# One block for experts and final sums, and three reorderings before it, in a streaming mixer and mixture-of-experts layer

## What is computed

```
m, s_h, s_r, buf = parallel_mixers(rmsnorm(h))     # HGRN2 scan + RWKV-7 scan, gated and added
h = h + m @ w_out
h = h + memory_cross_attention(rmsnorm(h), mem_k, mem_v)
h = h + hier_moe(rmsnorm(h))                       # best of 4 groups, then 2 of its 8 experts
y = rmsnorm(h)
```

## Time and profile before

| What | Value |
|---|---|
| median of 3 runs | 1563.61 us (1563.08 to 1565.07) |
| profiled execution: its time / its span | 1564.5 us / 1562.8 us |
| PE busy / PEld | 1418.8 us (91%) / 1183.2 us (76%) |
| DVE / ACT / POOL busy | 644.7 us (41%) / 576.9 us (37%) / 150.2 us (10%) |
| mean granted TensorE clock | 0.955 of full speed |

### The profile page before, as it was taken

The page is one execution under the profiler, slowest core; times in us unless marked ns, Lnnn a source line. Parts: engine busy times, 40 slices in busy tenths (PEclk is TensorE's granted clock), DMA queues, the critical chain, the costliest instruction groups (busy, mean ns, idle before and its releaser), DMA issues. The chain is left out here.

```text
span 1562.8 us, 35890 instructions
## 1 busy us (share of the span) xinstructions
PE 1418.8 (91%) x16169; PEld 1183.2 (76%) x16169; DVE 644.7 (41%) x955; ACT 576.9 (37%) x813; POOL 150.2 (10%) x265
## 2 busy tenths in 40 slices
PE   4899999897999999799999979999998599999980
PEld 3899999887999999699999969998887233333330
DVE  4333333573566566434445436532333222222224
ACT  4454554421656665324343364433325000000002
POOL 1000000100200010000000000000000133333410
PEclk8899999998999999899999989999998699999995
DMA  4233333301233232300000142562213699999834
GB/s 160 55 95 81 91 86 85 99 2 48 80 87 86 81 101 81 108 4 10 4 4 4 49 144 80 172 183 69 82 55 135 255 398 400 377 392 390 331 117 180
DMA packets 168271, 205.56 MB, mean 132 GB/s; under 512 B 24477, under 2 KB 148086, under 8 KB 155574
## 3 DMA queue, kind: packets, MB, share of 16 engines
q1 hardware_dynamic: 152722, 187.72, 35.2%
q0 software_dynamic: 15088, 15.46, 3.0%
q10 hardware_dynamic: 308, 0.09, 0.0%
HBM read 242.55 MB, written 27.23 MB: 173 GB/s over the span
## 5 line engine op out<-in xcount | busy, mean ns | idle before, releaser
L273 PE MATMUL ps<-rounded,w_hi 128*128 128x272 f32 (+1 forms) x1200 | 351.4, 293 | 23.6 <-DVE w_lo L262 16.6
L274 PE MATMUL ps<-rounded,w_hi 128*128 128x272 f32 (+1 forms) x1200 | 349.2, 291 | 0.0
L275 PE MATMUL ps<-rounded,w_lo 128*128 128x272 f32 (+1 forms) x1200 | 348.3, 290 | 0.0
L273 PEld LDWEIGHTS ps<-rounded,w_hi 128*128 128x128 f32 (+1 forms) x1200 | 227.7, 190 | 30.8 <-issue 30.3
L275 PEld LDWEIGHTS ps<-rounded,w_lo 128*128 128x128 f32 (+1 forms) x1200 | 227.3, 189 | 0.3
L274 PEld LDWEIGHTS ps<-rounded,w_hi 128*128 128x128 f32 (+1 forms) x1200 | 226.9, 189 | 0.6
L262 DVE TENSOR_TENSOR w_lo<-ring,w_hi 128x1024 fp32r<-128x1024 f32 (+1 forms) x75 | 90.7, 1214 | 181.7 <-ACT w_hi L257 181.7
L257 ACT CAST w_hi<-ring 128x1024 fp32r<-128x1024 f32 (+1 forms) x75 | 77.6, 1038 | 147.9 <-DMA ring<-in_w_in 147.8
L1497 PE MATMUL ps<-rounded,d_high 128*128 128x272 f32 x384 | 114.7, 299 | 6.7 <-DVE rounded L1417 5.8
L1498 PE MATMUL ps<-rounded,d_high 128*128 128x272 f32 x384 | 112.7, 294 | 0.0
L1499 PE MATMUL ps<-rounded,d_low 128*128 128x272 f32 x384 | 112.3, 293 | 0.0
(11 more groups left out here) (411 smaller groups left out, 2312.7 us busy)
## 6 DMA issues: line engine op xcount, KB each, us to landing
ring<-in_w_in SPq DMA_DIRECT2D x74, 512.0 KB, 3.9
arena<-in_expert_w_gate SPq DMA_DIRECT2D x32, 1024.0 KB, 8.0
arena<-in_expert_w_up SPq DMA_DIRECT2D x32, 1024.0 KB, 10.4
arena<-in_expert_w_down SPq DMA_DIRECT2D x32, 1024.0 KB, 10.4
arena<-in_w_out SPq DMA_DIRECT2D x8, 512.0 KB, 4.6
arena<-in_wk_x SPq DMA_DIRECT2D x8, 512.0 KB, 3.9
arena<-in_wv_x SPq DMA_DIRECT2D x8, 512.0 KB, 4.1
arena<-in_wq_x SPq DMA_DIRECT2D x8, 512.0 KB, 3.9
```

What stands on the lines that cost most here:

```text
L273: pe.matmul(out, w_hi[j][:, k, 0:m], xh, start=(k == 0), stop=False)
L274: pe.matmul(out, w_hi[j][:, k, 0:m], xl, start=False, stop=False)
L275: mm = pe.matmul(out, w_lo[j][:, k, 0:m], xh, start=False, stop=(k == FT - 1))
```

## The change

Five edits:
- **Scan end.** In the last scan step ScalarE copies u0 before it does `rstd` of the chunk before. After the scan, the transposed end state goes to PSUM bank 4 in place of bank 0, TensorE then does the first half of dense unit 1 before it waits for the last chunk, and ScalarE copies the end state before it splits the last chunk.
- **Norm factors.** The memory norm, "x" and "f" are now one Sqrt on ScalarE and a reciprocal on VectorE; a one-element Sqrt after attention has the table loaded there.
- **Token counting.** `count_tokens` stands after the third `turn_row` in TensorE's order, not after the fifth.
- **First gathers.** The three gathers leave the long block (with GpSimd's wait for `x_out`) and open GpSimd's part of the expert block.
- **One block.** The final block's work follows the expert work in the same block: no `end_stage` between, and SP, not GpSimd, waits for the scatters.

```diff
@@ scan_act
-            if i >= 1:
+            if i >= 1 and nxt:
                 rstd(act, i - 1)
             if cur:
                 keep_bank("r_u0_done", n, C_B, u0_s, "r_u0")
-                if not nxt:
-                    for u in range(1, HIS):
-                        d_hi(act, u)
+            if not nxt:
+                rstd(act, i - 1)
+                for u in range(1, HIS):
+                    d_hi(act, u)
@@ d_unit
             if u == 1:
                 pe.wait_ge(S["r_st0"], K)
-                pe.wait_ge(S["r_state_turned"], 2)
+                d_steps(pe, u, 1).then_inc(S["d_prod"], 1)
+                return
@@ norm factors
-        def token_rstd(act, rs, b, name):
+        def token_rms(act, rs, b, name):
...
-                act.activation(dst, src, ACT.Ln, scale=1.0 / D, bias=eps).then_inc(S[name + "_ln"], 1)
-            act.wait_ge(S[name + "_ln"], 2)
-            for dst, src, eps in parts:
-                act.activation(dst, dst, ACT.Exp, scale=-0.5).then_inc(S[name + "_rs"], 1)
+                act.activation(dst, src, ACT.Sqrt, scale=1.0 / D, bias=eps).then_inc(S[name + "_rms"], 1)
+
+        def token_inverse(dve, rs, name):
+            dve.wait_ge(S[name + "_rms"], 2)
+            for m, ts in ((P, slice(0, TT - 1)), (DEC, slice(TT - 1, TT))):
+                dve.reciprocal(rs[0:m, ts], rs[0:m, ts]).then_inc(S[name + "_rs"], 1)
@@ long block, GpSimd
-                pool.wait_ge(S["x_out"], 16 * TT)
                 pool.wait_ge(S["x_from"], 1)
-                for i in range(XR):
-                    gather_x(pool, i)
@@ long block, ScalarE
                 rstd(act, K - 1)
+                act.wait_ge(S["r_end_turned"], 2)
+                act.copy(st_vk[1], heads(4)).then_inc(S["r_state_turned"], 1)
                 split_out_act(act, K - 1)
-                act.wait_ge(S["r_end_turned"], 2)
-                act.copy(st_vk[1], heads(Z_B)).then_inc(S["r_state_turned"], 1)
...
-                act.activation(mem_rs, mem_ss, ACT.Ln, scale=1.0 / D, bias=eps_c).then_inc(S["mem_ln"], 1)
-                act.wait_ge(S["mem_ln"], 1)
-                act.activation(mem_rs, mem_rs, ACT.Exp, scale=-0.5).then_inc(S["mem_rs"], 1)
+                act.activation(mem_rs, mem_ss, ACT.Sqrt, scale=1.0 / D, bias=eps_c).then_inc(S["mem_rms"], 1)
...
                         attention_act(act)
+                        act.activation(tiny[:, 3:4], eps_c, ACT.Sqrt)
@@ long block, TensorE
                 pe.wait_ge(S["r_st"], K)
+                turn_heads(pe, 4, st_p).then_inc(S["r_end_turned"], 1)
+                pe.wait_ge(S["d_lo"], 2)
                 pe.wait_ge(S["r_z"], K)
-                turn_heads(pe, Z_B, st_p).then_inc(S["r_end_turned"], 1)
+                d_steps(pe, 1, 0)
                 pe.wait_ge(S["r_out_lo"], K)
                 d_steps(pe, 0, 1).then_inc(S["d_prod"], 1)
...
-                for t in range(TT):
+                for t in range(3):
                     turn_row(pe, t)
                 count_tokens(pe)
+                for t in range(3, TT):
+                    turn_row(pe, t)
@@ long block, VectorE
                 split_out_dve(dve, K - 1)
+                dve.wait_ge(S["mem_rms"], 1)
+                dve.reciprocal(mem_rs, mem_rs).then_inc(S["mem_rs"], 1)
...
+                        token_inverse(dve, x_rs, "x")
...
+                token_inverse(dve, f_rs, "f")
@@ expert block
             def _(sp):
...
+                for j in range(2):
+                    sp.wait_ge(S[f"m_out{j}"], 16 * (PAIRS // 2))
+                for t in range(TT):
+                    m = tokens(t)
+                    sp.dma_start(res[t][0:m], y_picks.rearrange("(k n) d -> n k d", k=TOP_K)[t * P:t * P + m]).then_inc(S[f"y_in{t}"], 16)
...
             def _(pool):
+                for i in range(XR):
+                    gather_x(pool, i)
...
                 scatter_y(pool, PAIRS - 1)
-                for j in range(2):
-                    pool.wait_ge(S[f"m_out{j}"], 16 * (PAIRS // 2))
...
-        S.end_stage()
-
-        with nc.Block() as block:
```

More of the change, by code:

```diff
@@ L1646, in att_out @@
             if t == 0:
-                pe.wait_ge(S["x_ln"], 2)
+                pe.wait_ge(S["x_rms"], 2)
             else:
@@ L1986, in _ @@
                         act.wait_ge(S["sq_summed"], 1)
-                        token_rstd(act, x_rs, 7, "x")
+                        token_rms(act, x_rs, 7, "x")
                 act.wait_ge(S["logits"], 1)
@@ L1990, in _ @@
                 act.wait_ge(S["sq_summed"], 2)
-                token_rstd(act, f_rs, 5, "f")
+                token_rms(act, f_rs, 5, "f")
                 act.wait_ge(S["f_rs"], 2)
@@ L2338, in keep_y @@
             dve.tensor_copy(y_b[i % 2].rearrange("p (c n) -> p c n", c=2), ps[:, 5:7, :]).then_inc(S["m_y"], 1)
+        froom = Room(flat[:, 0:B4 * BW], B4 * BW)
+        res = [froom.take(TOP_K, D) for _ in range(TT)]
+        y_sq, ss, rstd = froom.take(D), froom.take(TT), froom.take(TT)
         with nc.Block() as block:
@@ L2348, in _ @@
                         load_part(sp, u - 2, "d")
+                for j in range(2):
[3 more added lines that the diff above has]
+                    sp.dma_start(res[t][0:m], y_picks.rearrange("(k n) d -> n k d", k=TOP_K)[t * P:t * P + m]).then_inc(S[f"y_in{t}"], 16)
+                for t in range(TT):
+                    sp.wait_ge(S["y_done"], t + 1)
+                    dst = O["y_prompt"][0, t * P:(t + 1) * P, :] if t < TT - 1 else O["y_sample"][0]
+                    sp.dma_start(dst, h_tok[0:tokens(t), t, :]).then_inc(S["y_out"], 16)
+                sp.wait_ge(S["y_out"], 16 * TT)
             @block.gpsimd
             def _(pool):
+                for i in range(XR):
+                    gather_x(pool, i)
                 for i in range(PAIRS):
@@ L2371, in _ @@
                     keep_h(act, i)
+                for t in range(TT):
+                    m = tokens(t)
+                    act.wait_ge(S["y_sum"], 2 * t + 2)
+                    act.activation(y_sq[0:m], h_tok[0:m, t, :], ACT.Square, accum_out=ss[0:m, t:t + 1]).then_inc(S["y_ss"], 1)
+                    act.wait_ge(S["y_ss"], t + 1)
+                    act.activation(rstd[0:m, t:t + 1], ss[0:m, t:t + 1], ACT.Sqrt, bias=eps_c[0:m], scale=1.0 / D).then_inc(S["y_rms"], 1)
             @block.tensor
@@ L2396, in _ @@
                     keep_y(dve, i)
-        S.end_stage()
-        froom = Room(flat[:, 0:B4 * BW], B4 * BW)
-        res = [froom.take(TOP_K, D) for _ in range(TT)]
-        y_sq, ss, rstd = froom.take(D), froom.take(TT), froom.take(TT)
-        with nc.Block() as block:
-            @block.gpsimd
-            def _(pool):
-                pass
-            @block.vector
-            def _(dve):
                 dve.wait_ge(S["slot_gain_in"], 16)
@@ L2431, in _ @@
                                                  op0=ALU.mult, op1=ALU.mult).then_inc(S["y_done"], 1)
-            @block.scalar
-            def _(act):
-                for t in range(TT):
-                    m = tokens(t)
-                    act.wait_ge(S["y_sum"], 2 * t + 2)
-                    act.activation(y_sq[0:m], h_tok[0:m, t, :], ACT.Square, accum_out=ss[0:m, t:t + 1]).then_inc(S["y_ss"], 1)
-                    act.wait_ge(S["y_ss"], t + 1)
-                    act.activation(rstd[0:m, t:t + 1], ss[0:m, t:t + 1], ACT.Sqrt, bias=eps_c[0:m], scale=1.0 / D).then_inc(S["y_rms"], 1)
-            @block.sync
-            def _(sp):
-                for t in range(TT):
-                    m = tokens(t)
-                    sp.dma_start(res[t][0:m], y_picks.rearrange("(k n) d -> n k d", k=TOP_K)[t * P:t * P + m]).then_inc(S[f"y_in{t}"], 16)
-                for t in range(TT):
-                    sp.wait_ge(S["y_done"], t + 1)
-                    dst = O["y_prompt"][0, t * P:(t + 1) * P, :] if t < TT - 1 else O["y_sample"][0]
-                    sp.dma_start(dst, h_tok[0:tokens(t), t, :]).then_inc(S["y_out"], 16)
-                sp.wait_ge(S["y_out"], 16 * TT)
 _INS = ["x_prompt", "x_sample", "mem_prompt", "cache_mem_k", "cache_mem_v", "state_hgrn", "state_rwkv", "state_rwkv_shift",
```

## The result

The changed kernel takes 1550.98 us (median of 4 runs, 1549.71 to 1552.09), the kernel before 1563.34 us on the same chip (1562.69 to 1565.07): ratio 0.9919, 95% interval 0.9902 to 0.9936. It is faster, by 12.4 us where 15.6 were forecast (1548.0, range 1541.5 to 1554.5). The profiled execution took 1550.33 us, its span is 1548.5, 14.3 less than before.

A forecast was written before the change was run, and what follows sets the result against it. TensorE was taken to set the pace between four places of waiting; -5.75 - 3.4 + 3.0 - 9.5 = -15.65 us from the median of 1563.61 gave 1548.0 us, range 1541.5 to 1554.5.

The forecast's parts named there:

- Scan end: End of the scan: earlier second correction and unit 1 matmuls done inside TensorE's wait, together -5.75 us.
- four places: Scan end, router, border to the experts and border behind them: -5.75, -3.4, +3.0 and -9.5 us.
- Rival 1: Border to the experts: first gather lands as in a quiet stretch, -0.8 for +3.0, 1544.2 us; chance 0.17.
- rival 2: Router block's end: GpSimd's drain of 6.9 us stays though the gathers leave, 1552.6 us; chance 0.15.
- rival 3: First expert pairs: TensorE starts at half clock and stays there, slower, 1592 us with four pairs; chance 0.03.
- the order: Last scan step: u0 copied before `rstd` brings the second correction and everything to the last chunk's split 2.7 us earlier.
- unit 1's half: Scan end: 24 matmuls of dense unit 1 hidden in TensorE's wait for the last chunk's split, 3.05 us.
- Router: Router: norm factor starts VectorE's chain 1.3 us earlier, counting starts after three row tiles; together -3.4 us up to VectorE's end.
- The "bounds" of -1.3 to -4.0: Router: -1.3 if the count gains no more than VectorE's chain, -4.0 if counting is also half a microsecond faster.
- Border to the experts: Start of expert block: drain gone, 6.4 us earlier, but gathers exposed, 0.8 + 8.6 = 9.4 us; net +3.0.
- estimate of 6.5 us: Border to the experts: gather landing time if DMA engines alternate queues; net 0.9, whole sum 2.1 us better; not adopted.
- Border behind the experts: Border before the final sums: load of picked outputs issued 9.5 us earlier, 7.65 of it GpSimd's drain; -9.5 us.

The follow-up runs named there:

- experiment 2: Kernel before, with only the last scan step changed: ScalarE copies u0 ahead of `rstd`, weight splits follow; ratio 0.9979 to the kernel before, 1560.52 us.
- experiments 5 and 7: Changed kernel with counting behind all five row tiles again, 1555.08 us; changed kernel with router norm factor as Ln and Exp with two table loads again, 1550.52 us.
- experiment 6: Changed kernel plus 24 transposes with unread results on TensorE between third row tile and counting; 1551.07 us, ratio 0.9914 to the kernel before.
- experiment 4: Changed kernel, with SyncE's first expert-block loads issued only when the first two gathers have landed; 1547.02 us, ratio 0.9903 to the kernel before.
- experiment 1: Kernel before, with only the final sums moved into the expert block and SyncE waiting for the scatters; 1555.06 us, ratio 0.9945.
- gathers_back: Changed kernel, with the first three gathers and GpSimd's wait for `x_out` back in the long block; 1547.56 us, ratio 0.9899 to the kernel before.
- rows_first: Changed kernel, with token counting behind all five row tiles again; 1555.08 us, ratio 0.9942 to the kernel before.
- busy_wait: The kernel of experiment 6: changed kernel plus 24 transposes with unread results ahead of the counting; 1551.07 us, ratio 0.9914.

## Why the prediction was right, and where it was off

The forecast held in its sum: each of the four places moved in the direction given, three of them for the reason given and to within 1.0 us, and none of the rivals came. The fourth, the router, lost most of its gain. That the total is only 2.4 us short of the forecast (13.2 for 15.65) owes 1.25 us to a place priced at nothing; that part is luck. Rival 1 (the quiet landing) is refuted by landings of 9.1 us and more; rival 2 (the drain stays) by the drain of 40 ns; rival 3 (experts at half clock) by the expert stretch, 275.83 against 275.84.

- *Scan end*, -5.75 forecast, -6.05 measured. Both parts were right by themselves: the order -2.60 for -2.7 (experiment 2), unit 1's half -3.10 for -3.05. The clock did fall again, as assumed, but a little less: the 48 matmuls behind the wait took 7.63 us where they had taken 7.99. The memory norm kept its cover: its scaling ends at 930.89, the transposes start at 933.03.
- *Router*, -3.4 forecast, -0.54 measured. This is the term that was mis-sized. The counting did start 3.27 us earlier behind the transposed logits, as forecast (3.4). But "for all that follows" took the counting at the 5.0 us that it had before; it took 7.7, since TensorE ran at 1.2 GHz through it. Of the two edits that bring the start forward, the earlier place of the counting kept its gain. The new norm factor lost its own: with it the counting is slow in either order, and this part of the router is longer than without it (experiments 5 and 7). Filling the wait of 3.30 us ahead of the counting brings back 2.9 us (experiment 6), so the clock can be held there; why the norm factor moves the moment of its fall stays open. The "bounds" of -1.3 to -4.0 took the counting only as faster, never as slower; the window at 0.59 behind the scan's wait was the warning.
- *Border to the experts*, +3.0 forecast, +4.0 measured. To the first turn it was +3.4 (12.55 for 9.13): the landing took 9.1 us where I took 8.6. The rest is 0.2 for the second turn, which waited 1.59 us for its gather where it had waited 1.41 for VectorE, and 0.3 for a first product that took 8.31 us where it had taken 7.98. Rival 1, the quiet landing, failed because of the weight loads alone (experiment 4). By the rule of the Trainium skill on DMA engines that go round their queues (DMA: Bandwidth & Descriptors, "Queues, rings and completion order") the prediction had an estimate of 6.5 us; the three gathers of the changed kernel took 9.1, 11.3 and 13.6.
- *Border behind the experts*, -9.5 forecast, -9.51 measured, alone -9.0 by the medians (experiment 1).
- *Not forecast*: -1.25 in the dense units, which goes with another moment of the clock's fall; the new order of u0 and `rstd` alone had it too (experiment 2).

The sum of the stretches is -13.2 us, the medians say -12.4.

## What to carry to other kernels

Price work behind a wait on TensorE at the low clock as well as at the high one, also when the wait itself is not new: an edit on another engine can move the moment at which the clock falls, and an edit that only brings a start forward can then cost time. Where the wait cannot go, work whose result nobody needs can keep the clock up. It did so ahead of the counting; ahead of the listing it ran past the wait's end and lost part of the gain, and ahead of the first expert product it gained nothing. When a transfer is moved behind a border, look at what else starts there: two waits that put SyncE's loads (four of 1 MB and one of 0.5 MB) behind two gathers gave back as much as the move had cost (4.2 us for 4.0). Compare stretches between landmarks, not end times, when the code ahead of a change scatters as much as the step is worth.

## What was not expected of the hardware

- GpSimd's drain at the end of a block with gathers lasts until 0.2 us after the last of them has landed (1230.7 and 1230.5 before, 1221.8 and 1221.6 in `gathers_back`); without them it is 40 ns. Behind the experts it is longer than that: it begins at 1517.1 and takes 9.11 us, while the last scatter, issued at 1517.34, lands after 3.2. Why is not shown.
- With the same code up to there, the table load near 873 lies between 871.03 (`gathers_back`) and 874.74 (`rows_first`) from profile to profile. Executions of one and the same program differ as well (`busy_wait` by 8.5 us over six runs); how much of the difference near 873 belongs to the program can't be told from one profile of each.
